# The first two weight blocks of a decoder layer: worked on together, chunk by chunk, and loaded in quarters

## What is computed

```
h = rmsnorm(x, g_mix)                       # per token
z = h @ w_in                                # 1024 x 2048: q, k, v, two LRU inputs, three short-conv inputs
a, b, c = attention(q, k, v), rglru(...), short_conv(...)
x = x + concat(rmsnorm(a), rmsnorm(b), rmsnorm(c)) @ w_out
up = rmsnorm(x, g_ffn) @ w_up               # 1024 x 5632
x = x + (silu(conv3(gate)) * conv3(u)) @ w_down
```

## Time and profile before

| what | value |
|---|---|
| median of 3 runs | 1156.15 us |
| lowest and highest | 1152.42 and 1158.8 us |
| the profiled execution's own time | 1154.53 us |
| its span in the profile | 1152.8 us |
| PE (TensorE) busy | 1120.6 us, 97% of the span, 7032 matmuls |
| DVE (VectorE) busy | 799.0 us, 69% |
| ACT (ScalarE) busy | 327.7 us, 28% |
| POOL (GpSimd) busy | 77.8 us, 7% |

### The profile page before, as it was taken

How to read it: one execution, slowest core, us unless ns; L and a number is a source line. 1 busy time by engine, 2 the same in 40 slices (tenths; PEclk the granted TensorE clock), 3 DMA queues, 4 the chain that set the end, 5 groups by cost and what they waited for, 6 DMA issues and landing times.

```text
span 1152.8 us, 18167 instructions
## 1 busy us (share of the span) xinstructions
PE 1120.6 (97%) x7032; PEld 1084.8 (94%) x7032; DVE 799.0 (69%) x1505; ACT 327.7 (28%) x524; POOL 77.8 (7%) x54
## 2 busy tenths in 40 slices
PE   7999999998999999999999999999999999999896
PEld 7899988877999999999999999999999999999894
DVE  6954668997997876667666667666756756575757
ACT  7344335665454421111112111111111111111222
POOL 0311110101342000000000000000000000000000
PEclk9999989999999999999999999999999999999898
DMA  6310210114343111111111111111111111111004
GB/s 243 109 38 24 92 38 19 38 56 168 128 147 120 46 38 55 37 55 36 55 36 55 50 41 48 43 55 36 49 42 55 36 55 39 52 36 55 19 15 147
DMA packets 25178, 72.17 MB, mean 63 GB/s; under 512 B 3472, under 2 KB 10000, under 8 KB 25104
## 3 DMA queue, kind: packets, MB, share of 16 engines
q1 hardware_dynamic: 24992, 71.45, 18.0%
q10 hardware_dynamic: 144, 0.15, 0.1%
HBM read 66.76 MB, written 5.87 MB: 63 GB/s over the span
## 4 chain that ended last, share of the span: by engine, by line
PE 71%; DVE 2%; ACT 1%; issue 1%; POOL 0%; DVEq 0%; ACTq 0%
PE psum L1466 63%; PE psum L1672 5%; PE psum L1497 2%; PE psum L1718 1%; DVE h_lo L1114 0%; ACT w_hi L531 0%; DVE x_sb L1378 0%; ACT act_hi L531 0%; PE psum L1549 0%; DVE zb L1374 0%; DVE zb L822 0%; ACT h_hi L638 0%; POOL act_lo L484 0%; DVE x_sb L1159 0%; DVE x_sb L1290 0%
## 5 line engine op out<-in xcount | busy, mean ns | idle before, releaser
L1466 PE MATMUL psum<-h_hi,w_hi 128*128 128x344 f32 x1248 | 406.6, 326 | 1.4 <-DVE zb L850 1.4
L1466 PE MATMUL psum<-h_lo,w_hi 128*128 128x344 f32 x1248 | 398.6, 319 | 0.0
L1466 PE MATMUL psum<-h_hi,w_lo 128*128 128x344 f32 x1248 | 398.6, 319 | 0.0
L1466 PEld LDWEIGHTS psum<-h_hi,w_hi 128*128 128x128 f32 x1248 | 234.4, 188 | 5.5 <-issue 2.7
L1466 PEld LDWEIGHTS psum<-h_lo,w_hi 128*128 128x128 f32 x1248 | 234.4, 188 | 2.6
L1466 PEld LDWEIGHTS psum<-h_hi,w_lo 128*128 128x128 f32 x1248 | 234.5, 188 | 0.0
L531 ACT ACTIVATE w_hi<-raw 128x1024 fp32r<-128x1024 f32 x94 | 99.3, 1058 | 443.1 <-PE psum L1466 432.6
L1290 DVE TENSOR_TENSOR x_sb<-psum,x_sb 128x344 f32<-128x344 f32 x240 | 121.6, 514 | 81.5 <-PE psum L1466 81.4
L1466 PE MATMUL psum<-act_hi,w_hi 128*128 128x344 f32 x480 | 154.9, 323 | 2.9 <-DVE x_sb L1290 2.9
L1466 PE MATMUL psum<-act_hi,w_lo 128*128 128x344 f32 x480 | 155.3, 324 | 0.0
L1466 PE MATMUL psum<-act_lo,w_hi 128*128 128x344 f32 x480 | 154.5, 322 | 0.0
(11 more groups left out here) (235 smaller groups left out, 1531.1 us busy)
## 6 DMA issues: line engine op xcount, KB each, us to landing
raw<-in_w SPq DMA_DIRECT2D x106, 512.0 KB, 3.2
x_sb<-in_x SPq DMA_DIRECT2D x8, 516.0 KB, 6.2
out_y<-x_sb SPq DMA_DIRECT2D x12, 344.0 KB, 2.4
x_sb<-in_x SPq DMA_DIRECT2D x2, 1376.0 KB, 11.5
x_sb<-in_x SPq DMA_DIRECT2D x4, 344.0 KB, 5.4
zb<-in_ck SPq DMA_DIRECT2D x1, 512.0 KB, 3.5
zb<-in_cv SPq DMA_DIRECT2D x1, 512.0 KB, 4.4
out_k_old<-in_k_keep SPq DMA_DIRECT2D x1, 508.0 KB, 5.9
```

Of the source, the lines that this page charges most:

```text
L1466: ins = mm(out, a, b, start=(at == 0), stop=(at == n - 1))
```

## The change

It does five things, all before job 6.

- SyncE and ACT load slots 0 and 1 in quarters of 256 columns (`part(p)`, two chunks each). ACT issues the first quarter of both; SyncE issues the other three between the quarters of x tile 0.
- x tile 1 comes in two transfers of four chunks each.
- ACT and DVE split slots 0 and 1 quarter by quarter, between the chunks of x tile 0.
- TensorE does jobs 0 and 1 together: for each chunk of x the three passes of slot 0, then the three of slot 1 (`first_pair`); the same for jobs 2 and 3, and 4 and 5. The six first jobs of the feed-forward part keep `first_job`.
- Ahead of everything TensorE does ten matmuls of `ones` by `ones`, 128 columns each, as soon as `ones` is set.

```diff
+WARM = 10
+def part(p):
+    return slice(2 * p * P, 2 * (p + 1) * P)
...
             for p in range(4):
                 k = slice(2 * p, 2 * p + 2)
                 sp.dma_start(x_sb[:, k, tile(0)], dram["x"][:, k, tile(0)]).then_inc(x0_landed[p], 16)
-                if p == 0:
-                    load_slot(0, Z_BLOCK[0])
-            load_slot(1, Z_BLOCK[1])
+                for s in range(2 if p else 0):
+                    sp.dma_start(raw[s][:, part(p)], w_dram[Z_BLOCK[s]][:, part(p)]).then_inc(
+                        raw_landed[s] if p == 3 else part_landed[p], 16)
             for t in range(1, NT):
-                sp.dma_start(x_sb[:, :, tile(t)], dram["x"][:, :, tile(t)]).then_inc(x_landed[t], 16)
+                if t == 1:
+                    sp.dma_start(x_sb[:, 0:4, tile(t)], dram["x"][:, 0:4, tile(t)]).then_inc(x1_landed, 16)
+                k = slice(4 if t == 1 else 0, KD)
+                sp.dma_start(x_sb[:, k, tile(t)], dram["x"][:, k, tile(t)]).then_inc(x_landed[t], 16)
...
             act.dma_start(const[:, :], dram["const"]).then_inc(const_landed, 16)
+            for s in range(2):
+                act.dma_start(raw[s][:, part(0)], dram["w"][Z_BLOCK[s]][:, part(0)]).then_inc(part_landed[0], 16)
...
-                    if t == 0 and k == 1:
-                        hi(0)
-                if t == 0:
-                    hi(1)
+                    if t == 0 and k % 2 == 0:
+                        for s in range(2):
+                            w = part(k // 2)
+                            if k == 6:
+                                act.wait_ge(raw_landed[s], 16)
+                            else:
+                                act.wait_ge(part_landed[k // 2], 32)
+                            nc.scalar.activation(split_hi[s][:, w], raw[s][:, w], ACT.Copy).then_inc(
+                                part_hi_ready if k < 6 else w_hi_ready, 1)
...
-            x_split(0, range(2))
-            w_lo_ffn(0)
-            x_split(0, range(2, 7))
-            w_lo_ffn(1)
-            x_split(0, range(7, KD))
+            for p in range(4):
+                x_split(0, range(2 * p, 2 * p + 1))
+                for s in range(2):
+                    dve.wait_ge(part_hi_ready if p < 3 else w_hi_ready, 2 * p + s + 1 if p < 3 else s + 1)
+                    V.tensor_tensor(split_lo[s][:, part(p)], raw[s][:, part(p)], f32(split_hi[s][:, part(p)]),
+                                    ALU.subtract).then_inc(part_lo_ready if p < 3 else w_lo_ready, 1)
+                x_split(0, range(2 * p + 1, 2 * p + 2))
...
+            def first_pair(t):
+                for k in range(KD):
+                    pe.wait_ge(h_ready, KD * t + k + 1)
+                    for s in range(2):
+                        if t == 0 and k % 2 == 0:
+                            pe.wait_ge(part_lo_ready if k < 6 else w_lo_ready, k + s + 1 if k < 6 else s + 1)
+                        wh, wl = wslot(s, k)
+                        out = first_ps[FIRST_JOBS.index((s, t))]
+                        mm(out, wh, h_hi[:, k, tile(t)], start=(k == 0), stop=False)
+                        mm(out, wh, h_lo[:, k, tile(t)], start=False, stop=False)
+                        ins = mm(out, wl, h_hi[:, k, tile(t)], start=False, stop=(k == KD - 1))
+                        if k == KD - 1:
+                            ins.then_inc(job_done, 1)
...
+            pe.wait_ge(consts_made, 1)
+            for n in range(WARM):
+                mm(task_ps[:, 0:P], ones[:, :], ones[:, :], start=True, stop=True)
             pe.wait_ge(consts_made, 4)
             for j in range(FILL_JOB0):
                 if j < len(FIRST_JOBS):
-                    first_job(j, 0, h_ready).then_inc(job_done, 1)
+                    if j % 2 == 0:
+                        first_pair(j // 2)
```

More of the change, by code:

```diff
@@ L338, in build @@
         side_ps = psum[:, 2 * 512:3 * 512]
+        part_landed = [sem(f"part_landed{p}") for p in range(3)]
+        x1_landed, part_hi_ready, part_lo_ready = sem("x1_landed"), sem("part_hi_ready"), sem("part_lo_ready")
         raw_landed = [sem(f"raw_landed{r}") for r in range(RAW)]
@@ L547, in _ @@
             for t in range(NT):
-                if t:
-                    act.wait_ge(x_landed[t], 16)
                 for k in range(KD):
@@ L552, in _ @@
                         act.wait_ge(x0_landed[k // 2], 16)
+                    if t == 1 and k == 0:
+                        act.wait_ge(x1_landed, 16)
+                    if (t, k) in ((1, 4), (2, 0)):
+                        act.wait_ge(x_landed[t], 16)
                     nc.scalar.activation(h_hi[:, k, tile(t)], x_sb[:, k, tile(t)], ACT.Copy,
                                          scale=gain_mix[:, k:k + 1]).then_inc(h_hi_ready, 1)
-                    if t == 0 and k == 1:
-                        hi(0)
-                if t == 0:
-                    hi(1)
+                    if t == 0 and k % 2 == 0:
[7 more added lines that the diff above has]
+                                part_hi_ready if k < 6 else w_hi_ready, 1)
                 if t == 1:
```

## The result

| | before | after |
|---|---|---|
| median of 6 runs | 1154.74 us (1152.42 to 1158.8) | 1163.45 us (1159.95 to 1164.48) |
| ratio | 1 | 1.0058, 95% interval 1.0043 to 1.0073 |
| profiled execution, own time | 1154.53 us | 1159.95 us |
| its span | 1152.8 us | 1157.9 us |

What follows compares the result with a forecast made beforehand. TensorE, busy 97% of the span, was taken as the bound. Terms -1.9 - 2.6 + 2.75 + 2.3 = +0.55 us on 1154.5 gave 1155.1, or 1156.7 from the median; forecast 1156 us, range 1151 to 1160.

Steps and rivals of the forecast that it cites:

- Where time can be won or lost: Whole kernel: TensorE bounds it, so time is won or lost where it idles or runs slow; at most 11.0 us.
- Start of the first pair: Kernel start: quarter loads and splits let the first real matmul begin at 6.5 instead of 8.42 us, gaining 1.9 us.
- The upper bound 6.95: Kernel start: latest time for the first real matmul if two weight quarters precede x's; the gain is then 1.5 us.
- The ones: Kernel start: ten matmuls of ones raise TensorE's clock during the initial wait, removing 20 slow starts, gaining 2.6 us.
- up or not up: First pair: clock up when it begins, gaining 2.6 us, or rising as late as today, gaining 0; failed ones 0.20.
- Feeding the pair, x tile 1 and the norm: During the pairs: loads, splits and the norm keep up with TensorE; cost nothing, at most 0.4 and 1 us.
- The wait before job 6: End of the pairs: TensorE waits for slot 2 to be split after job 4, costing 2.75 us, up to 3.3.
- A fall of the clock at job 6: Jobs 6 to 8: the wait before job 6 drops TensorE's clock, costing 2.3 us (0 to 9.3).
- The rival in which the clock holds: Wait before job 6: the clock stays up, net gain 1.75 us, 1152.8 us; chance 0.25.
- The wait before job 9 moves along with it: Before job 9: the 1.41 us wait keeps its length and shifts with the norm's matmul after job 7, adding nothing.
- The slow side: Jobs 6 to 8: half clock right through, 9.3 us less 1.75 won, +7.5, 1162 us; chance 0.05.
- From the profiled execution to the median: Whole kernel: the median before lies 1.6 us above the profiled execution, so the forecast counted from it is 1156.7 us.

Runs made afterwards that it cites:

- run 11: Changed kernel with jobs 4 and 5 apart, job 6 evicted earlier, first weight quarters issued by SyncE behind x's first quarter: 1154.63 us, ratio 0.9989.
- run 1: The changed kernel measured again, unchanged: 1162.04 us, ratio 1.0056 to the kernel before.
- run 5: Changed kernel with DVE's four small operations on the LRU constants moved behind evictions, ahead of that of job 9: 1158.66 us, ratio 1.0023.
- run 8: The kernel before with only the ten matmuls of ones added ahead: 1156.24 us, ratio 1.0003.
- run 13: Changed kernel with 13 matmuls of ones in the wait before job 6 and 8 before job 9: 1157.69 us, ratio 1.0023.
- run 12: run 11 with 14 matmuls of ones instead of 10 and DVE's small LRU operations later: 1153.74 us, ratio 0.9983.
- run 14: run 12 with DVE's writing of the padding moved ahead of the first reciprocal: 1153.37 us, ratio 0.9977.
- run 7: The kernel before with only DVE's eviction of job 6 moved ahead of the reciprocal of tile 2: 1155.95 us, ratio 1.0000.
- run 10: The kernel before with only jobs 4 and 5 paired, chunk by chunk: 1160.63 us, ratio 1.0044.
- run 2: Changed kernel with jobs 4 and 5 one after the other again: 1155.84 us, ratio 1.0005, one execution of 2220.86 us left out.
- run 9: Changed kernel in which POOL's w_lo of slot 4 also waits for DVE's eviction of job 6: 1161.46 us, ratio 1.0047.
- run 15: The changed kernel a third time, unchanged: 1158.31 us, a single execution.
- run 4: Changed kernel with slot 2 split into a third place, so its splitting need not wait for job 4: 1160.07 us, ratio 1.0043.
- run 3: Changed kernel with twelve matmuls of ones in the wait before job 6: 1159.61 us, ratio 1.0039.

## Why the prediction was wrong

- **Where time can be won or lost: right.** In the first profile nothing moved against the kernel before outside the start, the end of the pairs and the wait before job 9.
- **Start of the first pair, -1.9 (6.5 us): wrong by 1.4.** The upper bound 6.95, with two weight quarters ahead of x's, was reached by ACT only at its weight step, and PE began at 7.96. I had put the quarters behind x's piece, on a queue of their own, and then charged only for their bytes. x's quarter came as early as before (ACT at 4.78); the weights came 1.6 us after ACT wanted them. The rule of the Trainium skill, page "DMA: Bandwidth & Descriptors", section "Queues, rings and completion order", that the engines take turns among queues with work, points that way: the small pieces on ACT's queue shared with the large ones of SP. The trace agrees in this, that the same pieces issued next on SP's queue were used at 5.47 (run 11). It is argued and not shown: on ACT's queue the constants, used at 3.88, stood ahead of the pieces too, and no run separates the two.
- **The ones, -2.6: wrong by 1.5.** In the first profile the clock was up at the first real matmul, as forecast, and fell 1.4 us later; in runs 1, 5, 8 and 13 the first real matmul was already slow (0.42 to 0.43 us to the next start, 0.24 in the first profile). I had only two cases, up or not up, and missed the third: a fall while PE is already at work, after a pause of 2.26 us, longer than the 1.1 I had counted on because the start was late. Over all profiles: with pauses of 2.26 to 3.41 behind the ones 9 to 20 slow starts follow (9 in run 1, 18 in run 13, 20 in run 5), with pauses of at most 1.09 (runs 11, 12, 14) none. And the 20 of before are themselves not fixed: runs 7 and 10, which have no ones, show 14 and 18. So even the 1.1 of the ledger is partly the draw of that one execution, as run 8 with its 1.0003 says.
- **Feeding the pair, x tile 1 and the norm: nothing, right.** No wait of PE in the pairs.
- **The wait before job 6, +2.75 (up to 3.3): right in mechanism and bound**, 3.15 as measured. POOL's 2.85 for 2.40 is the difference. Run 10 shows the mechanism alone, run 2 its absence.
- **A fall of the clock at job 6, +2.3: right in mechanism, too large**: 1.5 in the ledger. It followed this wait in all six profiles in which it stood empty, at 2.79 to 3.43 us (the first, runs 1, 5, 9, 10, 15). The rival in which the clock holds fell with that.
- **"The wait before job 9 moves along with it": this step of the mechanism failed.** It counted that wait as a constant. It is 0.5 longer (1.92), and a wait of this length can bring its own fall of the clock: +0.43 and +1.5 in the profile, nothing of the kind in the sum. Run 2 shows the same place take back what the start won even where job 6 doesn't wait.
- **The slow side, 0.05 for 1162: the number was near, the mechanism not.** The clock did not stay down through jobs 6 to 8; it was back after ten to eleven starts and fell again at job 9's wait. What was missing is a case of two falls in one pass. With the measured sizes it gives -0.46 - 1.1 + 3.2 + 1.5 + 0.4 + 1.5 = +5.0, the ledger.
- **From the profiled execution to the median: open.** I counted on 1.6 us between them; they are 3.5 apart in the changed kernel. The filled waits do not explain it: the distance is 1.7 in run 13, but 1.5 in run 9, which has both waits empty, 5.2 in run 1 and 4.0 in run 7, which is the kernel before but for one eviction. The mean clock doesn't either (1159.95 and 1164.48 at the same 0.986). The differences among the three profiled executions of the changed kernel lie for the most part in the falls at job 9 and near 1090; all three lie below the median.

Which step failed, then, by size? The forecast was +0.55: 4.5 won at the start, 5.05 lost at the end of the pairs. The loss came out as forecast: run 10, which has it alone, is 4.4 per mille slower, 5.1 us. The gain did not come: run 2, which has all of the change but that loss, stands at 1.0005 (0.9992 to 1.0017) and not 4.5 us, 3.9 per mille, below the kernel before. Of the 4.5 us only 1.55 were there at the norm's matmul (the start won 0.46 and not 1.9, the ones 1.1 and not 2.6), and those were lost again at job 9, whose wait the forecast took for a constant. Runs 11 and 12 confirm the second half: the start won 3.8 and 4.0 us there at the same matmul, and 1.1 and 1.7 per mille arrived.

Open too: why DVE is idle for 0.54 us before its last small operation in the changed kernel and in run 4, with and without POOL at work.

## What to carry to other kernels

Pairing jobs to start sooner also makes them end together: look for whoever waits on the earlier of the two (here the buffer of slot 2), and pair only where nobody does; the first pairs could stay, the last could not. Price a new wait of TensorE twice, as idleness and as the slow starts behind it, and price again each existing wait that the change makes longer; matmuls of ones in the waits bought back more (3.3 per mille) than the whole start had won. And follow what is won at the start to the end before counting it: here the next wait on DVE or POOL took most of it back. When a first piece is to come sooner, try it on the same queue next in order rather than on a second queue; here that was 1.5 us sooner (5.47 for 6.95).

## What the runs showed of the hardware that was not expected

- **The clock falls after short waits, and not always after the same one.** Waits of PE in the first 60 us and what followed, over the profiles: 2.79 to 3.69, a fall each time (seven); 2.34 (run 11) none, 2.36 (run 12) a fall; 1.92 a fall in the first profile and none in run 1; 1.91 none in run 3, a fall in run 9; 1.91 a fall in run 15; 1.82 a fall in runs 2 and 14; 1.41 (before), 1.49 (run 10) and 0.74 (run 5) none. Late in the program: the wait of 2.17 of the earlier trace rows is followed by no fall before and in the first profile, but 2.16 at the same place is in run 12 (0.50 from 280 to 282), and the 1.7 near 1090 goes both ways. The slow starts after a fall of the first 60 us are ten to twelve, 1.3 to 1.5 us lost (10 to 12 times 0.129). The Trainium skill, page "TensorE: Matmul & The Clock Gate", section "Part 1: The HAM clock gate", says that the cold phase differs from run to run of one kernel; the profiles of the changed kernel agree (9 to 12 slow starts at the start in the first, run 1 and run 15; twelve, none and eleven after job 9).
- **The fall can come late.** In the first profile the eight starts after the pause of 2.26 and the eight after the wait of 1.92 are still fast (7.96 to 9.14; 52.27 to 53.45), and only then is the spacing 0.286; at job 6 of the same profile the first start is slow at once (36.73, the next at 37.19). A fast first matmul is no proof that the clock held.
- **A tiny operation can cost 2 us**: 128x2 in 2.04 (run 4), 128x24 in 1.35 (run 12), next to POOL's `w_lo`, for 0.17 elsewhere. Both stood ahead of an eviction that TensorE waited for. The kernel before has two such rows where TensorE waits for neither: a copy of 128x24 in 1.79 at 32.99, and one of 128x3 in 2.04 at 48.92, each beside POOL's `w_lo`.
